# Moving the FFN activations by 32, 96 or 224 bytes against the weights in on-chip memory

## The reference

```
def swiglu(h, w_gate, w_up, w_down):
    return (jax.nn.silu(h @ w_gate) * (h @ w_up)) @ w_down      # 1024 -> 2816 -> 1024, four times
```

## Time and profile before

| | |
|---|---|
| median of three runs | 2334.66 us (2327.92 to 2335.64) |
| the profiled execution's own time | 2331.55 us |
| its span, first to last instruction | 2329.8 us |
| mean granted TensorE clock | 0.991 |
| PE busy | 2269.9 us (97%) |
| DVE, ACT, POOL busy | 1105.4, 843.7, 1352.6 us |
| matmuls that read `act_high` or `act_low` | 1386 of 512 columns, 924 of 256 |

### The profile page before, as it was taken

One profiled execution on the slowest core, in us unless ns is written; L12 is line 12 of the kernel. 1 busy time (PEld: TensorE's weight loads), 2 busy tenths in 40 slices (PEclk: granted clock), 3 DMA queues, 4 the chain that ended last, 5 costly groups with the idle time before them and its releaser, 6 DMA issues.

```text
span 2329.8 us, 39284 instructions
## 1 busy us (share of the span) xinstructions
PE 2269.9 (97%) x13534; PEld 1997.9 (86%) x13534; DVE 1105.4 (47%) x2078; ACT 843.7 (36%) x1250; POOL 1352.6 (58%) x712
## 2 busy tenths in 40 slices
PE   8999999999999999999999999999999999998997
PEld 7988999888888888868888888888888988998997
DVE  6753468543765543267555422655522520245223
ACT  5454453544522212213322222422222423655653
POOL 6864788647665554403555443555544544468996
PEclk9999999999999999999999999999999999998998
DMA  8842468523365543301655433455533422224554
GB/s 290 272 145 73 136 230 290 185 80 124 121 226 198 197 143 100 115 31 55 226 180 201 158 93 98 172 202 194 190 92 96 167 91 100 97 98 150 188 180 135
DMA packets 112846, 356.58 MB, mean 153 GB/s; under 512 B 13168, under 2 KB 22896, under 8 KB 112368
## 3 DMA queue, kind: packets, MB, share of 16 engines
q1 hardware_dynamic: 112752, 355.31, 46.1%
HBM read 347.66 MB, written 1.05 MB: 150 GB/s over the span
## 4 chain that ended last, share of the span: by engine, by line
PE 82%; POOL 6%; DVE 4%; issue 4%; ACT 1%; DMA 1%; DVEq 0%; SPq 0%; POOLq 0%; ACTq 0%
PE ps L1861 22%; PE ps L1862 22%; PE ps L1863 22%; POOL w_low L1021 5%; PE ps L1992 2%; PE ps L2010 1%; PE ps L1912 1%; PE ps L1911 1%; PE ps L1910 1%; PE ps L2223 1%; PE ps L2319 1%; PE ps L2213 1%; DMA raw<-in_w_dram 1%; PE ps L2000 1%; DVE ps L1288 1%
## 5 line engine op out<-in xcount | busy, mean ns | idle before, releaser
L1021 POOL TENSOR_TENSOR w_low<-raw,w_high 128x1024 fp32r<-128x1024 f32 (+3 forms) x542 | 1204.5, 2232 | 685.5 <-ACT w_high L565 684.7
L565 ACT ACTIVATE w_high<-raw 128x1024 fp32r<-128x1024 f32 (+3 forms) x544 | 537.6, 990 | 1142.4 <-PE ps L1863 902.1
L1861 PE MATMUL ps<-h_high,w_high 128*128 128x256 f32 (+1 forms) x2720 | 892.4, 328 | 22.5 <-POOL h_low L1050 6.4
L1862 PE MATMUL ps<-h_low,w_high 128*128 128x256 f32 (+1 forms) x2720 | 882.3, 324 | 0.0
L1863 PE MATMUL ps<-h_high,w_low 128*128 128x256 f32 (+1 forms) x2720 | 882.1, 324 | 0.0
L1861 PEld LDWEIGHTS ps<-h_high,w_high 128*128 128x128 f32 x2720 | 515.7, 190 | 70.5 <-issue 9.2
L1863 PEld LDWEIGHTS ps<-h_high,w_low 128*128 128x128 f32 x2720 | 516.3, 190 | 42.8
L1862 PEld LDWEIGHTS ps<-h_low,w_high 128*128 128x128 f32 x2720 | 515.7, 190 | 42.6
L1861 PE MATMUL ps<-act_high,w_high 128*128 128x512 f32 (+1 forms) x770 | 266.2, 346 | 0.0
L1862 PE MATMUL ps<-act_low,w_high 128*128 128x512 f32 (+1 forms) x770 | 265.6, 345 | 0.0
L1863 PE MATMUL ps<-act_high,w_low 128*128 128x512 f32 (+1 forms) x770 | 265.6, 345 | 0.0
(11 more groups left out here) (213 smaller groups left out, 2332.0 us busy)
## 6 DMA issues: line engine op xcount, KB each, us to landing
raw<-in_w_dram SPq DMA_DIRECT2D x216, 512.0 KB, 3.5
raw<-in_wu_dram SPq DMA_DIRECT2D x176, 512.0 KB, 4.5
ada<-in_ada_dram SPq DMA_DIRECT2D x144, 512.0 KB, 4.0
raw<-in_wd_dram SPq DMA_DIRECT2D x64, 384.0 KB, 3.1
raw<-in_wd_dram SPq DMA_DIRECT2D x64, 320.0 KB, 2.9
raw<-in_wv_dram SPq DMA_DIRECT2D x24, 408.0 KB, 4.8
heads<-rot SPq DMA_DIRECT2D x96, 64.0 KB, 3.6
ada<-in_cond_dram SPq DMA_DIRECT2D x6, 512.0 KB, 5.0
```

The source lines that it names most:

```text
L565: e.activation(wh[:, c % RING, at_:at_ + w], raw[:, c % RING, 0:w], ACT.Copy).then_inc(hi_done, 1)
L1021: e.tensor_tensor(wl[:, c % RING, at_:at_ + w], raw[:, c % RING, 0:w], wh[:, c % RING, at_:at_ + w].bitcast(F32), ALU.subtract).then_inc(l ...
L1861: e.matmul(ps[:, bank, to:to + n], wh[:, j, w], hi, start=(first and t == tiles[0]), stop=False)
L1862: e.matmul(ps[:, bank, to:to + n], wh[:, j, w], low, start=False, stop=False)
```

## The change

The one pair of activation tensors becomes four pairs, one for each FFN, that lie over one another with starts moved by 32, 96, 224 and 32 bytes (`ACT_LINES`). Since the weights of down 0 to 2 are at the slot's start and those of down 3 are 64 bytes behind it, the distances become +32, +96, +224 (-32) and 32 - 64 = -32 (224). The two `ada2` rows of each FFN move with its tensors. Every instruction, wait and count stays as it is; addresses alone change.

```
+ACT_LINES = (32, 96, 224, 32)
...
-        a2 = Area(late)
-        ah = a2("act_high", [P, FT, 2 * T], F32R)
-        al = a2("act_low", [P, FT, 2 * T], F32R)
+        acts = []
+        for f, line in enumerate(ACT_LINES):
+            a2 = Area(late + line)
+            acts.append((a2(f"act_high{f}", [P, FT, 2 * T], F32R), a2(f"act_low{f}", [P, FT, 2 * T], F32R)))
...
-        ada2 = [at("ada2_0", [P, D], F32, late + tail),
-                at("ada2_1", [P, D], F32, late + size([P, FT, 2 * T], F32) + tail)]
+        ada2 = [[at(f"ada2_{f}_{q}", [P, D], F32, late + line + act_bytes * q + tail) for q in range(2)]
+                for f, line in enumerate(ACT_LINES)]
...
-                    e.tensor_tensor(flat(al, 2 * i + j // 2, 0, halves * T), hn[:, j // 2, 0:halves * T],
-                                    flat(ah, 2 * i + j // 2, 0, halves * T).bitcast(F32), ALU.subtract)\
+                    e.tensor_tensor(flat(acts[f][1], 2 * i + j // 2, 0, halves * T), hn[:, j // 2, 0:halves * T],
+                                    flat(acts[f][0], 2 * i + j // 2, 0, halves * T).bitcast(F32), ALU.subtract)\
...
-                    e.tensor_copy(flat(ah, 2 * i + j, 0, w), hn[:, j, 0:w]).then_inc(act_hi, 1)
+                    e.tensor_copy(flat(acts[f][0], 2 * i + j, 0, w), hn[:, j, 0:w]).then_inc(act_hi, 1)
...
-                return products(bank, j, range(DOWN[j]), sum(DOWN[0:j]), (ah, al), lo, w, j == 0, j == 3, None, lo,
+                return products(bank, j, range(DOWN[j]), sum(DOWN[0:j]), acts[f], lo, w, j == 0, j == 3, None, lo,
                                 LINE if f == 3 else 0)
```

More of the change, by code:

```diff
@@ L249, in program @@
         ada_prod = at("ada_prod", [P, D], F32, sq_at)
-        a2 = Area(late)
-        ah = a2("act_high", [P, FT, 2 * T], F32R)
-        al = a2("act_low", [P, FT, 2 * T], F32R)
+        acts = []
+        for f, line in enumerate(ACT_LINES):
+            a2 = Area(late + line)
+            acts.append((a2(f"act_high{f}", [P, FT, 2 * T], F32R), a2(f"act_low{f}", [P, FT, 2 * T], F32R)))
+            assert a2.at <= nc.sbuf_top
         tail = (FT - 2) * size([P, 2 * T], F32)
-        ada2 = [at("ada2_0", [P, D], F32, late + tail),
-                at("ada2_1", [P, D], F32, late + size([P, FT, 2 * T], F32) + tail)]
+        act_bytes = size([P, FT, 2 * T], F32)
+        ada2 = [[at(f"ada2_{f}_{q}", [P, D], F32, late + line + act_bytes * q + tail) for q in range(2)]
+                for f, line in enumerate(ACT_LINES)]
         a3 = Area(late)
@@ L272, in program @@
         dec = a4("dec", [P, 2, 4, T])
-        for a in (a1, a2, a3, a4):
+        for a in (a1, a3, a4):
             assert a.at <= nc.sbuf_top, (a.at, nc.sbuf_top)
@@ L521, in ffn @@
                     for q in range(2):
-                        e.dma_start(ada2[q][:, :], cond_d[:, q, :]).then_inc(cond_in, 16)
+                        e.dma_start(ada2[f][q][:, :], cond_d[:, q, :]).then_inc(cond_in, 16)
                     e.wait_ge(c_silu, 2 * LAYERS + 2 * f + 2)
@@ L528, in ffn @@
                             e.wait_ge(ada2_done, r + 1)
-                            e.dma_start(ada2[j % 2][:, :], ada_d[bass.ds(ADA_H + r, 1)].rearrange("a p n -> p (a n)"))\
+                            e.dma_start(ada2[f][j % 2][:, :], ada_d[bass.ds(ADA_H + r, 1)].rearrange("a p n -> p (a n)"))\
                                 .then_inc(ada2_landed[j % 2], 16)
@@ L871, in up @@
                     for q in range(2):
-                        e.activation(cond_bank(q), ada2[q][:, :], ACT.Silu).then_inc(c_silu, 1)
+                        e.activation(cond_bank(q), ada2[f][q][:, :], ACT.Silu).then_inc(c_silu, 1)
                 phase(base, *((WIDE, WD) if f < ADA_FFNS else (W8, WD_LAST)), silu, f < ADA_FFNS)
@@ L1237, in modulate, with modulate2 @@
                 e.wait_ge(ada_done, r + 3)
-            def modulate2(r, row, half):
+            def modulate2(f, r, row, half):
                 trash = sq[:, :, :].rearrange("p a t -> p (a t)")
                 e.wait_ge(ada2_landed[half], 16 * row + 16)
-                e.scalar_tensor_tensor(out=trash, in0=ada2[half][:, :], scalar=1.0, in1=cond_bank(0),
+                e.scalar_tensor_tensor(out=trash, in0=ada2[f][half][:, :], scalar=1.0, in1=cond_bank(0),
                                        op0=ALU.mult, op1=ALU.mult, accum_out=mod[:, bass.ds(ADA_H + r, 1), 0])\
@@ L1246, in modulate2 @@
                 e.wait_ge(ada_step, ADA_H + r + 1)
-                e.scalar_tensor_tensor(out=trash, in0=ada2[half][:, :], scalar=1.0, in1=cond_bank(1),
+                e.scalar_tensor_tensor(out=trash, in0=ada2[f][half][:, :], scalar=1.0, in1=cond_bank(1),
                                        op0=ALU.mult, op1=ALU.mult, accum_out=mod[:, bass.ds(ADA_H + r, 1), 1])\
@@ L1583, in up @@
                             for q in range(2):
-                                modulate2(ADA_F * f + RING * i + 2 * j + q, ADA_F // 2 * f + 2 * i + j, q)
+                                modulate2(f, ADA_F * f + RING * i + 2 * j + q, ADA_F // 2 * f + 2 * i + j, q)
                     for j in range(2):
```

## The result

The changed kernel is slower by 0.42%: the ratio of the runs is 1.0042 with a 95% interval of 1.0029 to 1.0054 (medians 2340.48 and 2329.3 us over 11 runs each). That is +9.8 us, 6.8 to 12.6. One run of the changed kernel took 10100.8 us and is not in the ratio; why it did is not known.

What follows compares the result with a forecast made beforehand. TensorE was taken to bound the down phases, matmuls times step. Terms +1.8, +0.6, -1.2 and +1.8 us gave +3.0: 2331.55 to 2334.6 us on the profiled execution, 2337.7 on the median's scale, stated as 2337; range 2322 to 2350.

Steps and rivals of the forecast that it cites:

- likeliest case: Down phases: small terms of the four FFNs that partly cancel, +3.0 us in sum, 2330 to 2343 us; chance 0.31.
- no measurable change: Whole kernel: time within about 0.3%, 7 us, of the kernel before; chance 0.44.
- What bounds the kernel: Four down phases: TensorE busy for the whole stretch, so time is number of matmuls times step; TensorE busy 97% of span.
- the four terms: Down phases, one term per FFN for its changed distance: +1.8, +0.6, -1.2 and +1.8 us, together +3.0 us.
- FFN 2: Down 2, distance -32: half of the way from 0 to -64, 2 ns less per matmul, -1.2 us.
- FFN 0: Down 0, distance +32: a third of the way from 0 to +96, 594 matmuls x 1 ns, +0.6 us.
- FFN 1: Down 1, distance +96: lower end of 3 to 7 ns more per matmul, 594 x 3 ns, +1.8 us.
- FFN 3: Down 3, distance -64 to -32: half of the way back from 113.3 to 120.0 ns, 528 x 3.3, +1.8 us.
- The cover in the up phases: Up phases: slower activation writes hidden by free engine time, thin only in up 3; costed at nothing, 3 us if writes lengthen.
- The upper end of the range: Down phases at worst: all 2310 matmuls take 6.7 ns more, +15.5 us; range reaches 2350 us.

Runs made afterwards that it cites:

- aligned run: Changed kernel with activations of FFNs 0, 1, 2 at 64, 128, 192 bytes from the weights' place, FFN 3 at 128; 2338.87 us, beside 2332.76 for the kernel before.
- the last run: Changed kernel with activations at the old place except down 2 (16 bytes), weights of downs 0 to 2 moved by 252, 240, 16; steps 226.7, 226.7, 230.0 ns, down 3 113.3.
- the version with the moved pieces: Activations at the old place; against the kernel before, remaining 256-column pieces (last output tile of downs 0-2, first three chunks of ups 0-2) get weights 64 bytes behind; ratio 0.9987.

## Why the prediction was right or wrong

The time, 2340.48, is inside the range of 2322 to 2350, and even inside the 2330 to 2343 of the likeliest case. The latter is luck: that case was +3.0 us on a median of 2334.66, and with eleven runs the kernel before has 2329.3, so a change of +9.8 lands where +3.0 was to land. The likeliest case was not what happened: I had no measurable change with 0.44, and the change is slower by more than 0.3%, which had 0.34.

What bounds the kernel: right. PE's busy time still equals the length of each down phase, and the difference is the number of matmuls times the step (11.3 us, where the ratio has 6.8 to 12.6). That made the working short, and it is why 6.7 ns could be read as 9.3 us. The 2.4 GHz named there is no more than the measured rate of the columns, 106.7 ns for 256, at a granted clock of 1.00; no run shows a frequency by itself. What failed is how the step was taken to depend on the distance: the four terms together were +3.0 us and measured 11.3.

FFN 2, at -32, is the term that failed in sign: -1.2 us forecast, 462 x 6.7 - 132 x 1.6 = +2.9 measured. I took half of the way from 0 to -64, but the gain at -64 was one of 256-column matmuls, and with 512 columns -64 itself costs 6.7 (233.3, aligned run, down 2). Gains of one width did not carry to the other; the table has 0 as the best place for 512 columns (226.7) and as one of the worst for 256 (119.9, where -64 has 113.5).

FFN 0 (+0.6 forecast, +2.7 measured) and FFN 1 (+1.8, +3.1): right in sign and too small. I interpolated as if the step were a smooth function of the distance with its minimum at 0. It jumps: at 32 bytes and more to either side the mean mostly lands 6.7 ns higher, at 233.3 (228.9 at +64, 230.0 at +80, 232.0 at -80, 234.3 at -96). For FFN 1 I had the very distance in the rows, took the lower end of 3 to 7 ns, and the upper end was it.

FFN 3: +1.8 forecast, 528 x 5.0 = +2.6 measured, inside what was said (113.3 to 120.0). But I put it down to the distance, and with the distance put back 117.8 of the 118.3 ns stayed; the cause of this term is open.

The cover in the up phases: right for this change. GpSimd's 739 ns for `act_low` in up 3 is 739 again, up 3 is 124.7 us for 124.8, and the run with the activations left in place shows no cost. VectorE's casts moved, but downwards, from 869 to 704 ns. (The 0.35 us that I quoted as GpSimd's wait for a cast was one case; over 20 of them it is 2.6 us, 0.13 each.)

```profile
L1115 POOL TENSOR_TENSOR act_low<-hn,act_high 128x256 f32 x20 | 14.8, 739 | 2.1 <-DVE act_high L1579 2.1
...
L1575 DVE CAST act_high<-hn 128x256 f32 x22 | 19.1, 869 | 3.3 <-DVE hn L1572 1.9
L1579 DVE CAST act_high<-hn 128x256 f32 x22 | 15.5, 704 | 3.3 <-DVE hn L1576 1.9
```

These are GpSimd's `act_low` in the changed kernel, then the casts before and in the changed kernel. Their length is no function of the activations' place alone. In the run with the distances -48, -80, +80 and -60 the activations lie as before, and yet the casts took 1397 ns, GpSimd waited 5.9 us for them instead of 2.6, and up 3 lasted 128.9 us instead of 124.8. That is what a thin cover would do, as the prediction had it; no run changed the casts alone, and what makes them long is open.

The upper end of the range, 2350, rests on +15.5 us, one step of 6.7 ns on all 2310 matmuls. No run shows such a rise for all of them. The 1386 of 512 columns did rise by it, to 233.3 in all three phases, but the halves gained in two of the three (116.7, 120.0 and 118.3 for 119.9) and down 3 rose by 5.0, so the whole came to 11.3. The 6.7 was the difference of two distances with 256 columns, and nothing in the rows said that 512 columns would rise by as much. A number that comes out right is no proof of its cause. It took the weights moved along to see that the distance costs here and not the place: activations on a multiple of 64 bytes cost as much at 128 and 192 (233.3), and 32 against 32 costs nothing (226.7).

The step of 512 columns rose from 226.7 to 233.3 ns with nothing but addresses changed, and fell back to 226.7 when the weights' addresses followed. What stays open is why. With 512 columns the step depends on where the two operands lie relative to each other within 256 bytes, for multiples of 32 (distance 0 at four places has 226.7 or 226.8, and -32 by either operand 233.3), and at 4 and 16 bytes on the moving operand's own start too (238.0 and 231.7 by the activations, 226.7 by the weights). With 256 columns even the same distance has two values, 113.3 and 117.8 at -64. That the weight load beside a matmul is what it meets fits down 0 of the run with `w_low` at -32, where the second matmul takes 239.7, and not down 1, where the second takes 229.2 and the third 235.8.

## What to carry to other kernels

Where TensorE's busy time is the length of a stretch, read its step from the timeline and multiply: here an address was worth 3% of the step (226.7 against 233.3 ns). For fp32r products choose the distance between moving and stationary operand by measurement, for each width on its own (here 226.7 ns at 0 for 512 columns, 113.3 at -64 for 256), and put several distances into one kernel's phases so that one run gives them all. Test a theory on alignment by moving both operands together (226.7 ns with both at 32 bytes); moving one changes place and distance at once (233.3).

## What the runs showed of the hardware

The mean step of 512, 504 and 496 columns comes out at 220.0, 226.7 and 233.3 ns again and again, whole multiples of 6.67 ns, even where single steps differ (230, 232 and 238 ns in down 1 of the changed kernel have the mean 233.36). But 228.9, 231.7, 238.0 and others occur as well, so it is a tendency and no rule.

With 256 columns the distance -64 has two states, 113.3 and 117.8 ns, each stable over 528 matmuls: down 3 had 113.3 before and with the weights at 64 in the last run but 117.8 with both moved by 32 bytes more. The place alone does not choose: in the version with the moved pieces both values occur in the same output tile, with the same places, 117.8 before four matmuls of other operands and 113.4 behind them. What chooses was not found; it is worth 2.4 us in down 3 alone, where the worst placement that was tried (w_high at -64, `w_low` at -32, 120.0) costs 3.5.
